# An encoder block on one core: VectorE makes the heads' w_in remainders, GpSimd adds the squares of a group's chunks up

## The reference, cut to what matters

```python
h = layer_norm(x, ln_emb_g, ln_emb_b)
z = h @ w_in[l]                                    # 1024 -> 3584 columns, 28 chunks of 128
xr, gate, cb, cc, cx = jnp.split(z, IN_SPLITS, axis=-1)
for d, pad in enumerate(LRU_PADS):                 # two directions
    xc = depthwise_conv(xr, lru_conv_w[l, d], pad) + lru_conv_b[l, d]
    hd = rg_lru(xc, ..., reverse=(d == 1))         # a linear recurrence along the tokens
    lru = hd if lru is None else lru + hd
y_lru = gelu(gate) * lru                           # 8 heads of 128 columns
y_conv = cb * depthwise_conv(cc * cx, conv_w[l], (1, 1))   # 4 chunks of 128 columns
mix = concat([rms_norm(y_lru, g1), rms_norm(y_conv, g2)])  # mean of squares over each group
h = layer_norm(ALPHA * h + mix @ w_out[l], ln1_g[l], ln1_b[l])
f = peer(h, ...)
h = layer_norm(ALPHA * h + f, ln2_g[l], ln2_b[l])
```

## Time and profile before

| what | us |
|---|---|
| runs, median of 3 (lowest to highest) | 1684.82 (1683.02 to 1686.22) |
| the profiled execution | 1688.24 |
| its span | 1686.1 |
| TensorE busy in the span | 1626.7 (96%) |
| VectorE busy | 1274.7 (76%) |
| GpSimd busy | 856.7 (51%) |
| ScalarE busy | 671.4 (40%) |

### The profile page before, as it was taken

The page is one execution under the profiler, slowest core; times in us unless marked ns, Lnnn a source line. Parts: engine busy times, 40 slices in busy tenths (PEclk is TensorE's granted clock), DMA queues, the critical chain, the costliest instruction groups (busy, mean ns, idle before and its releaser), DMA issues.

```text
span 1686.1 us, 23590 instructions
## 1 busy us (share of the span) xinstructions
PE 1626.7 (96%) x8590; PEld 1433.0 (85%) x8590; DVE 1274.7 (76%) x2484; ACT 671.4 (40%) x1100; POOL 856.7 (51%) x557
## 2 busy tenths in 40 slices
PE   7998889999999999999999989999999999999997
PEld 5876647799988999999999888888888888888885
DVE  6568878476989988946885267778777777888876
ACT  3557782333335333423333233333333333333332
POOL 5745434373556678867877224445555553222200
PEclk9999999999999999999999999999999999999999
DMA  7526301333446578797879989998999989999983
GB/s 261 162 82 199 116 7 41 122 98 119 129 142 205 153 222 226 227 320 209 239 209 283 328 308 322 319 325 308 339 323 323 318 295 350 352 351 358 352 268 112
DMA packets 242898, 397.17 MB, mean 236 GB/s; under 512 B 33704, under 2 KB 173408, under 8 KB 242784
## 3 DMA queue, kind: packets, MB, share of 16 engines
q1 hardware_dynamic: 182816, 259.17, 45.1%
q0 software_dynamic: 55296, 134.31, 26.7%
q10 hardware_dynamic: 4672, 2.19, 0.4%
HBM read 349.40 MB, written 46.20 MB: 235 GB/s over the span
## 4 chain that ended last, share of the span: by engine, by line
PE 79%; DVE 8%; ACT 5%; issue 2%; POOL 2%; DMA 2%; ACTq 0%; SPq 0%; DVEq 0%; POOLq 0%
PE bank L1788 30%; PE bank L963 28%; PE bank L951 6%; PE bank L780 5%; PE bank L1384 4%; PE bank L1662 3%; PE bank L839 2%; DVE hd L700 2%; DMA u_raw<-in_peer_u 2%; DVE dq L696 1%; POOL ut_lo L1003 1%; PE bank L1372 1%; ACT dw L558 1%; POOL rms L463 1%; ACT da L560 1%
## 5 line engine op out<-in xcount | busy, mean ns | idle before, releaser
L963 PE MATMUL bank<-xhi,ut_hi 128*128 128x384 f32 x1024 | 354.6, 346 | 0.3 <-ACT gel L989 0.3
L963 PE MATMUL bank<-xhi,ut_lo 128*128 128x384 f32 x1024 | 344.4, 336 | 0.0
L963 PE MATMUL bank<-xlo,ut_hi 128*128 128x384 f32 x1024 | 343.7, 336 | 0.0
L1130 POOL DMA_INDIRECT gathered<-in_peer_v,expert_rows x128 | 191.6, 1496 | 268.0 <-DVE gather_sum L1146 248.4
L1130 POOL DMA_INDIRECT gathered<-in_peer_u,expert_rows x128 | 168.2, 1314 | 177.9 <-DVE gather_product L1142 145.1
L234 POOL DMA_INDIRECT gate_matrix<-gate_values,gate_cells x128 | 219.6, 1716 | 58.4 <-issue 37.2
L1021 DVE TENSOR_TENSOR ut_lo<-bank,ut_hi 128x512 fp32r<-128x512 f32 x202 | 132.5, 684 | 151.7 <-ACT ut_hi L980 131.6
L1788 PE MATMUL bank<-v_hi,w_hi 128*128 128x512 f32 x760 | 237.9, 394 | 1.3 <-DVE w_lo L1900 1.3
L1788 PE MATMUL bank<-v_lo,w_hi 128*128 128x512 f32 x760 | 234.9, 390 | 0.0
L1788 PE MATMUL bank<-v_hi,w_lo 128*128 128x512 f32 x760 | 234.8, 390 | 0.0
L1833 ACT ACTIVATE v_hi<-gate_rows_then_feed 128x1024 fp32r<-128x1024 f32 x128 | 135.4, 1058 | 231.6 <-PE bank L1788 227.1
(11 more groups left out here) (248 smaller groups left out, 2634.9 us busy)
## 6 DMA issues: line engine op xcount, KB each, us to landing
u_raw<-in_peer_u SPq DMA_DIRECT2D x128, 512.0 KB
gate_rows_then_feed<-in_peer_v SPq DMA_DIRECT2D x128, 512.0 KB
gate_rows_then_feed<-gate_matrix SPq DMA_DIRECT2D x128, 192.0 KB
activations<-gel SPq DMA_DIRECT2D x96, 192.0 KB
gate_rows_then_feed<-activations SPq DMA_DIRECT2D x96, 192.0 KB
u_raw<-in_w_in SPq DMA_DIRECT2D x28, 512.0 KB, 4.8
gate_matrix<-gate_zeros SPq DMA_DIRECT2D x8, 1024.0 KB, 7.1
wq<-in_peer_wq SPq DMA_DIRECT2D x16, 512.0 KB, 4.3
```

The source lines that it names most:

```text
L963: ins = self.nc.tensor.matmul(self.bank[b + (r % 2) * spare][:, 0:DTOK], u[r % 2][:, k, :], x[:, k, 0:DTOK], start=(i == 0), stop=(i == 3 ...
L1130: self.nc.gpsimd.indirect_dma_start(out=self.tile[r][:, :], out_offset=None, in_=self.tables[kind], in_offset=bass.IndirectOffsetOnAxis(ap ...
```

## The change

- VectorE makes the remainder of chunk 1 too, behind its eight splits. GpSimd makes those of chunks 2 to 16 (`LOWER_BY_DVE = HX + 5`). VectorE makes 17 to 27: in head g one between the scan of the first direction and the product of the second, one behind the second scan.
- GpSimd's `head_output(g)` follows directly on the scans, for all 8 heads behind one another. It keeps a running total of the heads' squares: head 0's square is written into `sq[:, 1]`, each later one into `sq[:, 0]` and then added, one more operation for each head from 1 on.
- ScalarE writes the convolution's four squares into `th`, which the heads need later; GpSimd adds them up in three operations (`conv_squares`) behind chunk 14's remainder. ScalarE's first tanh of head 0 waits for that.
- TensorE sums each group's total once: the convolution's ahead of head 1's gates, the heads' before the last head's output product. 12 groups of four small matmuls become 2.

```diff
@@ gpsimd @@
             eng.wait_ge(y_ready, i + 1)
-            eng.wait_ge(sums_done, i - 1)
-            G.tensor_tensor(out=sq[:, i % 2, :], in0=y[:, g, :], in1=y[:, g, :], op=ALU.mult).then_inc(sq_ready, 1)
+            eng.wait_ge(sums_done, 1)
+            G.tensor_tensor(out=sq[:, int(g == 0), :], in0=y[:, g, :], in1=y[:, g, :], op=ALU.mult).then_inc(sq_ready, 1)
+            if g:
+                eng.wait_ge(sq_ready, i + 1)
+                G.tensor_tensor(out=sq[:, 1, :], in0=sq[:, 1, :], in1=sq[:, 0, :], op=ALU.add).then_inc(total_ready, 1)
+                eng.wait_ge(total_ready, g + 1)
+
+        def conv_squares():
+
+            eng.wait_ge(sq_ready, CONV)
+            for i in range(2):
+                ins = G.tensor_tensor(out=sq[:, i, :], in0=th[:, i, 0, :], in1=th[:, i, 1, :], op=ALU.add)
+            link(ins)
+            G.tensor_tensor(out=sq[:, 0, :], in0=sq[:, 0, :], in1=sq[:, 1, :], op=ALU.add).then_inc(total_ready, 1)
+            eng.wait_ge(total_ready, 1)
...
-        eng.wait_ge(w_lo_ready, 1)
-        w_lower(1)
+        eng.wait_ge(w_lo_ready, 2)
...
-        for n in range(HX, len(order)):
+        for n in range(HX, LOWER_BY_DVE):
             w_lower(n)
-            if (n - HX) % 2 == 0 and n > HX + 4:
-                head_output((n - HX - 6) // 2)
-        for g in range(HEADS - 3, HEADS):
+            if n == HX + 2:
+                conv_squares()
+        for g in range(HEADS):
             head_output(g)
@@ scalar @@
-            after(eng, sums_done, i - 1)
-            S.activation(sq[:, i % 2, :], y[:, made[i], :], ACT.Square).then_inc(sq_ready, 1)
+            S.activation(th[:, i // 2, i % 2, :], y[:, made[i], :], ACT.Square).then_inc(sq_ready, 1)
...
+                if g == 0:
+                    eng.wait_ge(total_ready, 1)
@@ vector @@
         def w_lower(n):
             eng.wait_ge(w_hi_ready, n + 1)
+            after(eng, w_lo_ready, n)
...
         for k in range(KD):
             turner.split(eng, k)
-
-
+        w_lower(1)
...
                                            data1=dq[:, d, along], initial=0.0, op0=ALU.mult, op1=ALU.add)
+                if d == 0 and LOWER_BY_DVE + 2 * g < len(order):
+                    w_lower(LOWER_BY_DVE + 2 * g)
             link(ins)
             V.sem_inc(scan_ready, 1)
+            if LOWER_BY_DVE + 2 * g + 1 < len(order):
+                w_lower(LOWER_BY_DVE + 2 * g + 1)
@@ tensor @@
-            eng.wait_ge(sq_ready, i + 1)
-            conv = made[i] >= HEADS
+            eng.wait_ge(total_ready, (HEADS, 1)[i])
...
-            if j > 1:
-                sum_squares(j - 2)
...
-            sum_squares(CONV - 2 + g)
+            if g == 1:
+                sum_squares(1)
             head_gates(g)
...
-                sum_squares(MIX - 2)
-                sum_squares(MIX - 1)
+                sum_squares(0)
```

More of the change, by code:

```diff
@@ L341, in mixer @@
     dve_chain, pool_chain, act_chain = sem("dve_chain"), sem("pool_chain"), sem("act_chain")
-    closing_chain = sem("pool_chain_closing")
+    closing_chain, total_ready = sem("pool_chain_closing"), sem("square_totals_ready")
     chunk_used, wo_hi_ready, wo_lo_ready, y_hi_ready, y_lo_ready = (sem(n) for n in (
@@ L374, in mixer @@
     made = list(range(HEADS, MIX)) + list(range(HEADS))
+    LOWER_BY_DVE = HX + 5
     last = slice((TB - 1) * P, T)
@@ L718, in vector @@
             wo_lower(i)
-        eng.wait_ge(sums_done, MIX)
+        eng.wait_ge(sums_done, 2)
         for i in range(2):
@@ L796, in sum_squares @@
         def sum_squares(i):
-            eng.wait_ge(sq_ready, i + 1)
-            conv = made[i] >= HEADS
+            eng.wait_ge(total_ready, (HEADS, 1)[i])
             for tb in range(TB):
-                at = int(conv) * TB + tb
-                ins = mm(bank[2][:, at:at + 1], sq[:, i % 2, tb * P:(tb + 1) * P], ones[:, 0:1],
-                         start=(i == 0 and tb == 0), stop=(i == MIX - 1 and tb == TB - 1))
+                at = i * TB + tb
+                ins = mm(bank[2][:, at:at + 1], sq[:, 1 - i, tb * P:(tb + 1) * P], ones[:, 0:1],
+                         start=(i == 1 and tb == 0), stop=(i == 0 and tb == TB - 1))
             ins.then_inc(sums_done, 1)
```

## The result

| | before | after |
|---|---|---|
| median of the runs | 1684.14 us (4 runs, 1683.02 to 1686.22) | 1664.36 us (4 runs, 1664.14 to 1664.58) |
| ratio, with 95% interval | 1 | 0.9878, 0.9856 to 0.9899 |
| profiled execution, span | 1688.24 us, 1686.1 us | 1664.14 us, 1662.3 us |
| last split of the start (VectorE) | 26.50 us | 23.75 us |
| first tanh of head 0 | 108.87 us | 103.85 us |

The medians differ by 19.8 us; by the ratio the gain is 20.5 us, 17.0 to 24.3 by its interval. The forecast was a gain of 17.0 us and 1668 us, with a range of 1663 to 1676: the time is inside the range, and the gain was forecast some 3 us too small. The first split of the input starts at 16.42 us in the kernel before and at 15.69 in the kernel after, ahead of anything that was edited: 0.73 us of every later difference between the two columns are that.

A forecast was written before the change was run, and what follows sets the result against it. Bounds: TensorE in the convolution stage, a ScalarE-VectorE ring in the heads, with VectorE waiting for GpSimd's remainders. 1.7 + 2.4 + 2.9 + 11.1 - 1.05 = 17.0 us off the median 1684.82: forecast 1668 us, range 1663 to 1676.

The forecast's parts named there:

- start and square sums, to the first tanh: Up to head 0's first tanh: 1.7 us from chunk 1's remainder on VectorE, 2.4 us from square sums leaving TensorE.
- head 0: First product to second scan's end falls from 7.99 to 5.0 us in head 0; 2.9 us taken as gain.
- heads 1 to 5: Four turns of heads 1 to 4 gain 2.64 us each, head 5 gains 0.5; together 11.1 us.
- last scan to powers: Mixer's end: GpSimd's added add meets VectorE's operations and takes one slot, costing 1.05 us.
- The ring: Heads: ScalarE's tanh to root, VectorE's product and two scans, ScalarE again; a turn falls from 18.74 to 16.1 us.
- The start: Splits and chunk 1: one cast no longer meets GpSimd's remainder, TensorE begins chunk 1 at 26.35; gain 1.7 us.
- The square sums: Convolution stage: three groups of 0.79 us leave TensorE's row, 2.4 us on the path; GpSimd's three adds stay hidden.
- the rest of the span unchanged: Sign to look for: rms powers start 17 us earlier, and everything behind them in the span stays as before.
- VectorE first at the port: Rival, 12%: remainder behind the second scan takes 1.21 us and the late add costs nothing; gain 19.9 us, 1665.
- VectorE's row is fuller: Rival, 16%: remainder between the scans also meets something, up to 1.3 us in six heads; gain 9.2 us, 1675.6.
- The load is only moved: Rival, 4%: VectorE loses as much by its new work as it did by waiting, and 1685 us stays.
- TensorE at its low clock: Rival, 3%: TensorE falls to 1.2 GHz in the heads, 28 us a turn; 40 us more at full price, 1725.

The follow-up runs named there:

- e5: Kernel after, with GpSimd's output of a head waiting until VectorE has made the remainder behind the scan; 1663.57 us, ratio 0.9873 to the kernel before.
- e11: Kernel after, run again without an edit; 1664.98 us, ratio 0.9882 to the kernel before.
- e3: Kernel before, with only chunk 1's remainder moved to VectorE behind the splits; 1682.55 us, ratio 0.9986.
- e1: Kernel before, run again without an edit; 1685.22 us, ratio 1.0002.
- e2: Kernel before, with only the remainders of chunks 17 to 27 on VectorE and heads' outputs directly behind the scans; 1671.73 us, ratio 0.9922.
- e4: Kernel before, with only the squares added up on GpSimd and two groups of sums on TensorE; 1681.47 us, ratio 0.9976.
- e7: Kernel after, without GpSimd's add for the last head; TensorE sums that square itself, eight small matmuls instead of four; 1663.77 us, ratio 0.9874.
- e8: Kernel after, with the edits of e5 and e7 and VectorE's mean squares after four pairs of remainders instead of five; 1660.32 us, ratio 0.9852.
- e12: The kernel of e8, run again unchanged; 1661.07 us, ratio 0.9858 to the kernel before.
- e6: Kernel after, with both remainders of a head behind its second scan and none between the scans; 1672.14 us, ratio 0.9921.
- e10: Kernel after, plus unused GpSimd memsets, which only write SBUF, at the moments when it made remainders before; 1665.23 us (1 run).
- e9: Kernel after, plus unused GpSimd subtractions, which read SBUF twice, at the moments when it made remainders before; 1689.58 us (1 run).

## Why the prediction was right, and where it was short

Step by step, the kernel after against the earlier trace rows:

| step | forecast gain, us | traced, us |
|---|---|---|
| start and square sums, to the first tanh | 1.7 + 2.4 = 4.1 | 5.02 (4.29 from the first split) |
| head 0 | 2.9 | 3.01 |
| heads 1 to 5 | 11.1 | 10.81 |
| last scan to powers | -1.05 | -1.21 |
| to the start of the powers | 17.05 | 17.63 (16.89 from the first split) |

*The ring.* Right in mechanism and size. Second product 0.68 (0.7 forecast), second scan 1.22 (1.22), first product to the end of the second scan 4.92 (5.0), remainder behind the scan 2.27 to 2.36 (2.28), end of scan to first product 146.92 - 135.83 = 11.09 (11.1), turn 16.01 to 16.10 (16.1) in heads 2 to 4. The 0.4 us by which head 1 was longer is one DMA issue of ScalarE, which the sum had not priced: 1.26 us instead of 0.49, less the third of a microsecond that ScalarE has to spare. In e5, where it has none, a like issue cost 0.75 us. That VectorE ends the turn by a third of a microsecond was right: e5 took 1.06 us off the remainder, the turn fell by 0.3 to 0.4 us, and ScalarE became the later one by 0.78.

*The start.* The term of 1.7 us was right. TensorE began chunk 1 at 25.64, not 26.35, and 2.40 us earlier than before (28.04); but 0.73 us of that are that the first split itself began at 15.69 instead of 16.42. This is scatter of the start and no part of the gain: the first split is at 16.77 in e11 and at 15.96 in e3. Counted from the first split, chunk 1 begins 25.64 - 15.69 = 9.95 us in, where it was 28.04 - 16.42 = 11.62: 1.67 us. 2.0 us are won at the cast that no longer meets GpSimd, and a part goes to the wait for chunk 1's remainder, as the sum had it. The first tanh stands 88.14 to 88.16 us behind the first split in the nine profiled executions that have all of the start's and the squares' edits, and 92.45 to 92.59 in before, e1 and e2.

*The square sums.* 3 x 0.79 = 2.4 us were on the path and are gone (what is left of the 4.29 us is 2.62; e4, with this part alone, has 2.7), and the three adds (94.75 to 98.68 in the kernel after) were hidden as said: the row of 14 chunks has no gap.

*Behind the powers.* The step that failed is "the rest of the span unchanged". The two profiled executions differ by 17.6 us at the start of the powers and by 23.8 us in the span, so 6.2 us come from work in which nothing was edited. Some 1.6 us of them stand at one place. Stretches of 6 us in the output projection, the kernel before and then the kernel after:

```profile
276.00:282.00 6.00, 6.00 (x20) 4.70 (x19) 5.00 (x6) 0.00 (x0) 3.07 (x3) 0.72 0.00 0
```

```profile
258.00:264.00 6.00, 5.99 (x26) 4.88 (x27) 4.99 (x5) 0.00 (x0) 3.10 (x3) 1.00 0.00 0
```

The mean granted clock was 0.72 in the one, because for 3.4 us of it the lower level (1.2 GHz) was granted, and 1.00 in the other; TensorE got through 20 instructions instead of 26. TensorE had sat idle ahead of it in both, for 1.83 us in the kernel before and for 2.60 us in the kernel after, and behind the same 2.6 us the low level did come in e1, e2 and e4. Laying the same instructions of ScalarE side by side, two more steps stand where the kernel before has a low-clock stretch and the kernel after has none, 1.6 us behind 546.5 and some 1.2 us behind 952.7; the other 1.8 us are in smaller steps, the largest some 1.2 us, beside which no low clock stands.

The profiled execution of the kernel before, 1688.24 us, lies 4.1 us above the median of its runs, 1684.14, so most of the 6.2 us belong to that one execution. What is left is between the runs and the sum: 19.8 us in the medians (20.5 by the ratio) against the 16.9 to 17.3 us that the traces show at the powers, counted from the first split. That is some 3 us; the lower ends of the two intervals, 17.0 us and, in e11, 16.9, just reach the traced figure. Taken in the same way, 1685 us times one less the ratio, less what the powers' start shows, the excess was 3.7 us in the kernel after, 2.9 in e11, 2.5 in e4, 3.0 in e5, 3.2 in e7, 3.4 in e8, 3.2 in e12, 0.8 in e6, 1.4 in e3 and -0.6 in e2. Each has 2 to 4 us of uncertainty, but seven of the eight comparisons with the squares' part have 2.5 us or more, and e2 and e3, which lack it, have less. So it may be something in that part, and e6 speaks against it; no run tests it, and the cause stays open. With this excess the time is only just inside the forecast's own bounds, 1664 to 1672.

*The rivals.* "VectorE first at the port" did not happen in the kernel after: GpSimd's output at 119.52 was ahead of VectorE's remainder at 119.60. e5 made it happen: 15.68 us a turn, where the rival's 1.8 us over five turns come to 15.74. "VectorE's row is fuller" did not happen: the remainder between the scans took 1.20 us in every head. "The load is only moved", behind which stood the Trainium skill (Perfetto Trace Analysis, Optimizing Scalar/DVE Operations), fell too: the operation costs VectorE 1.20 us where it runs alone, and it cost VectorE a wait of 2.1 us when GpSimd ran it; e6 shows when it would come true, with all of it placed where GpSimd reads. "TensorE at its low clock" had 3%: the granted clock over the heads was 0.99, up from 0.95.

## What to carry to other kernels

When a two-input VectorE row is longer than the same row elsewhere, look at what GpSimd reads beside it: moving that operation to VectorE can be worth more than its length there (1.2 us on VectorE, against 2.1 us of waiting on the chain). Put it where GpSimd does not read, and where both start together let the one on the path go first (e5). When two traces are compared, count from a landmark ahead of the edits: here the first split's start scattered by 1.6 us over fourteen profiled executions, and the stretch from it to the first tanh by 0.02 us over nine. A sum made from one profiled execution should leave a few us for the part of the span that nobody touched.

## What the runs showed of the hardware

*GpSimd's powers can be shut out for a whole row.* Two powers of 128 x 4 took 12.96 to 13.03 us together beside VectorE's last seven pairs of remainders, the first 11.97 to 12.04 and the second 1.01, in twelve profiled executions. They took 3.53 us, 1.94 and 1.62, beside its last eight (e8, e12). In e11 the last pair ended at 252.81 + 0.54 = 253.35, the first power at 254.24 and the second at 255.23; in the kernel before it was 269.56 + 0.54 = 270.10, 270.99 and 271.98. So the first power, by its end, came through only when VectorE's two-input row was over, 0.89 us behind it in both. Why it gets in when the row is one pair longer isn't shown; that it does was the same in two executions.

*A memset does not hold VectorE up.* 128 x 1024 in 0.95 us beside scan and remainder, with none of them longer (e10); a subtraction of the same size cost them 2.1 us each (e9).

*The lower clock level comes and goes at places that come back.* In the kernel before and in e1, the same code, TensorE's lower level was granted for 3.4 us at 160.8, 198.3, 276.8, 546.5, 952.7 and 993.6 us (and for 6.8 at 225.6) in the one, and at 23.4, 180.4, 218.0, 228.2, 276.0 and 317.0 (and for 6.8 at 989.4) in the other. Each stands behind an idle stretch of TensorE. Counted from the powers' start, one begins 725 to 735 us in, behind 4.1 us of idle time, in all fourteen profiled executions. Others come at the same few places in some executions and not in others: 16 to 18 us in, behind 1.8 to 2.6 us of idle time, in before, e1, e2 and e4 alone; 56 to 58 us in, behind 1.4 us, in eight of the fourteen. So a single trace is no basis for a term of a few us at such a place.
